# A hybrid decoder layer: stick quarters given out after the front step and after the rear step of each slot, in lumps of half the size

## What is computed

```
xn = RMSNorm(h); P = xn @ W_in
group A (RWKV-7, 8 heads x 64), for each token t:
    sa = S @ (-kk_t)
    S  = S * w_t + sa (kk_t * a_t)^T + v_t k_t^T
    y_t = S @ r_t
group B (stick-breaking, 8 heads x 64), for each block of 128 queries:
    z = q k^T / sqrt(64)
    A[t,s] = beta[t,s] * prod_{s<j<t} (1 - beta[t,j]), s < t, beta = sigmoid(z)
    o = A @ v
h += RMSNorm(concat(A, B) @ W_out)
h += RMSNorm(relu(RMSNorm(h) @ W_up)^2 @ W_down)
```

## Time and profile before

| | |
|---|---|
| median of 3 runs | 1838.2 us (1837.49 to 1838.92) |
| profiled execution | 1837.52 us, span 1835.6 us |
| PE busy | 1701.7 us, 93% of the span |
| DVE busy | 825.3 us, 45% |
| ACT busy | 699.3 us, 38% |
| POOL busy | 507.9 us, 28% |
| granted TensorE clock, mean | 0.968 |

### The profile page before, as it was taken

How to read it: one execution, slowest core, us unless ns; L and a number is a source line. 1 busy time by engine, 2 the same in 40 slices (tenths; PEclk the granted TensorE clock), 3 DMA queues, 4 the chain that set the end, 5 groups by cost and what they waited for, 6 DMA issues and landing times. The chain is left out here.

```text
span 1835.6 us, 36078 instructions
## 1 busy us (share of the span) xinstructions
PE 1701.7 (93%) x14676; PEld 1420.1 (77%) x14676; DVE 825.3 (45%) x1125; ACT 699.3 (38%) x1222; POOL 507.9 (28%) x523
## 2 busy tenths in 40 slices
PE   4999999969799999999992996999999999999998
PEld 4999999957677777877761784888888888888886
DVE  5132433325355455556549343444444444444436
ACT  5253443426456456555554343222121221212212
POOL 6332433304234333334425343111111111111110
PEclk7999999979899999999996997999999999999999
DMA  3336255341310300301012223211111111111104
GB/s 140 111 113 211 100 179 198 138 125 62 74 31 17 88 17 16 89 17 30 17 50 100 81 92 109 63 46 46 55 60 46 46 46 46 57 46 46 46 24 161
DMA packets 60890, 139.38 MB, mean 76 GB/s; under 512 B 5713, under 2 KB 32849, under 8 KB 60769
## 3 DMA queue, kind: packets, MB, share of 16 engines
q1 hardware_dynamic: 57024, 123.80, 21.0%
q10 hardware_dynamic: 3744, 13.85, 1.9%
HBM read 100.06 MB, written 37.57 MB: 75 GB/s over the span
## 5 line engine op out<-in xcount | busy, mean ns | idle before, releaser
L1722 POOL TENSOR_TENSOR ffn_ul<-ffn_relu,ffn_uh 128x512 fp32r<-128x512 f32 x64 | 82.8, 1294 | 576.2 <-ACT ffn_uh L1694 576.2
L1751 DVE TENSOR_TENSOR all_acc<-all_acc,ffn_down 128x512 f32<-128x512 f32 x240 | 161.2, 685 | 121.9 <-PE ffn_down L1798 121.3
L618 PE MATMUL inproj_acc<-xn_xh,inproj_wh 128*128 128x346 f32 (+1 forms) x624 | 207.4, 332 | 8.4 <-DVE inproj_wl L539 8.4
L1790 PE MATMUL ffn_up<-all_mh,ffn_wuh 128*128 128x512 f32 x512 | 200.1, 391 | 12.0 <-DVE ffn_wul L1734 12.0
L618 PE MATMUL inproj_acc<-xn_xh,inproj_wl 128*128 128x346 f32 (+1 forms) x624 | 201.1, 322 | 0.0
L618 PE MATMUL inproj_acc<-xn_xl,inproj_wh 128*128 128x346 f32 (+1 forms) x624 | 201.0, 322 | 0.0
L1798 PE MATMUL ffn_down<-ffn_wdh,ffn_uh 128*128 128x512 f32 x512 | 200.0, 391 | 0.0
L1790 PE MATMUL ffn_up<-all_ml,ffn_wuh 128*128 128x512 f32 x512 | 199.8, 390 | 0.0
L1790 PE MATMUL ffn_up<-all_mh,ffn_wul 128*128 128x512 f32 x512 | 199.6, 390 | 0.0
L1798 PE MATMUL ffn_down<-ffn_wdh,ffn_ul 128*128 128x512 f32 x512 | 199.4, 389 | 0.0
L1798 PE MATMUL ffn_down<-ffn_wdl,ffn_uh 128*128 128x512 f32 x512 | 199.2, 389 | 0.0
(11 more groups left out here) (244 smaller groups left out, 3442.8 us busy)
## 6 DMA issues: line engine op xcount, KB each, us to landing
ffn_raw_u<-in_w_up SPq DMA_DIRECT2D x32, 512.0 KB, 3.6
ffn_raw_d<-in_w_down SPq DMA_DIRECT2D x32, 512.0 KB, 4.2
xn_raw<-in_w_in SPq DMA_DIRECT2D x28, 512.0 KB, 4.6
p_scratch<-inproj_out ACTq DMA_DIRECT2D x26, 520.0 KB, 2.7
chunk_scratch<-inproj_fields SPq DMA_DIRECT2D x4, 2720.0 KB, 9.2
inproj_rkv<-p_scratch SPq DMA_DIRECT2D x14, 520.0 KB, 4.5
mix_fld<-chunk_scratch SPq DMA_DIRECT2D x17, 384.0 KB, 3.7
mix_fld<-chunk_scratch SPq DMA_DIRECT2D x17, 256.0 KB, 2.9
```

The costliest lines, as they stand in the source:

```text
L618: last = pe.matmul(acc[g][:, 0:size], w[s][:, kt, :], xx[:, kt, col:col + size], start=(kt == 0 and j == 0), stop=(kt == KD - 1 and j == 2))
L1722: pool.tensor_tensor(ul[s][:, f, cols], relu[j % 2][:, :], uh[s][:, f, cols].bitcast(F32), ALU.subtract).then_inc(u_low.sem, 1)
L1751: dve.tensor_tensor(part, part, downs[o % 4][:, :], ALU.add).then_inc(added.sem, 1)
L1790: last = pe.matmul(ups[j][:, :], w[f][:, k, :], xx[:, k, cols], start=(k == 0 and jj == 0), stop=(k == KD - 1 and jj == 2))
```

## The change

The quarters are given out after the front step and again after the rear step of each slot. There are twice as many lumps, of 1 or 2 quarters each (528 quarters over 288 half-slots). The same instructions are issued by each engine; only their order changes, and only on PE, ACT and DVE.

```
                 for _ in range(LAP_SLOTS):
-                    next(ahead, None)
-                    next(behind, None)
-                    k += 1
-                    due = k * quarters // slots
-                    for _ in range(due - given):
-                        next(sticks)
-                    given = due
+                    for part in (ahead, behind):
+                        next(part, None)
+                        k += 1
+                        due = k * quarters // (2 * slots)
+                        for _ in range(due - given):
+                            next(sticks)
+                        given = due
```

## The result

The changed kernel takes 1860.66 us (median of 4 runs, 1859.04 to 1863.29) against 1838.3 us before, a ratio of 1.0123 with a 95% interval of 1.0106 to 1.0141: 22.4 us slower. The forecast was 1866.2 us, 28 us slower, with 1854 to 1879 us as the range. Its profiled execution took 1859.04 us.

A forecast was written before the change was run, and what follows sets the result against it. PE was taken to bound the mixing stage. Profiled 1837.5 us, plus 37.1 for switches, less 9.1 for mix_a waits, DMA waits 0, gave 1865.5, and with 0.7 us 1866.2 us; range 1854 to 1879 us for 8 in 10.

The forecast's parts named there:

- The bound: Mixing stage: only PE is near its limit, busy 533.2 of 573.0 us, so its own time sets the stage.
- 109 added round trips: PE's order in the mixing stage: unbroken runs of 64-row matmuls go from 143 to 252.
- 0.34 us a trip: PE going from 128-row to 64-row matmuls and back: 0.34 us each, +37.1 us in all.
- The edges-alone case: PE's switches: only the two edges count, 0.19 us a trip; 1849.8 us in all, chance 6%.
- the rival by which handoffs were the bound: Mixing stage: apparent switch cost is handoff latency that finer order hides; faster, 1824.6 us, chance 3%.
- Waits for mix_a, -9.1 us: PE's waits for DVE's mix_a in the mixing stage: two thirds of 13.6 us go; bounds 0 and 13.6.
- The other reason: Mixing stage: half-lumps keep some matmuls between a tri sum and the rest sum needing its exponent; part of the 9.1 us.
- DMA waits, 0: PE's two stalls on loads of mix_vt for new pairs: no change, bounds -1 to +2 us.
- Lock-step lag: Mixing stage: DVE and ACT empty the rear bank later, 119 rear steps 0.1 us late each; 1878.1 us, chance 7%.
- the clock: PE in the mixing stage: many small gaps bring its clock down for a tenth of it; 1891 us, chance 5%.

The follow-up runs named there:

- the stage that held only this: Kernel before with a PE-only stage in front: 60 alternations of 64-row with 128-row matmuls took 20.93 us more than kind by kind.
- The two cuts of the lump: Kernel before with whole-tick lumps on all engines, ending after the tri sum or after the rest sum: 1845.89 us and 1845.43 us.
- the fewest trips: Kernel before with quarters given only after every second slot on all engines, 72 round trips: 1884.45 us.

## Why the prediction came out as it did

- **The bound.** Right: PE's own time sets the mixing stage, and outside of it nothing changed: the stage is 22.0 us longer and the span 21.6.
- **109 added round trips.** Right. Alone, 63 of them and 109 of them gave a loss in step with their number, and from ACT's and DVE's new order with PE's old to the changed kernel, which differ in PE's order alone, it is 32.7 us, 0.30 us a trip, with the waits that change beside them in it.
- **0.34 us a trip.** Right: 0.35 us in the stage that held only this, 0.355 in the row after. The edges-alone case (0.19) is out, and so is the rival by which handoffs were the bound (under 0.125). By the rule of the Trainium skill, TensorEngine Tiling (Array Packing), Key Properties, a change of tiling mode drains TensorE; the stage agrees, 0.35 us for a change of mode and under 0.01 for a change of matrices within one.
- **Waits for mix_a, -9.1 us.** About right, or up to 3 us too small; the forecast's distance of 5.5 us from the result lies here and in small waits that the sum put at nothing. The sum took two thirds of the matmuls' 13.6 us. But a matmul's modelled end lies 0.16 us beyond the start of the next in an unbroken stream (0.28 against 0.12 us for the L1232 at 934.14), so each wait loses that much in the table and short ones are not in it at all: the weight loads show 33 waits where the matmuls show 22. The loads' 24.4 us are somewhat too many, since they hold idle time that a load has without a wait too. A third reading takes starts: the distance from the matmul before, less the shortest that the same pair has in any of these runs at the same clock. These are 19.3 us in the same 33 places before and 10.4 in 16 after, 8.9 less. The matmul behind a wait is slow besides: from the one at 914.64 it is 0.34 us to the next start and not 0.23. PE's next row before:

```profile
914.98 0.39 PE L1218 MATMUL mix_cb<-mix_wsl,mix_rest_r 128*128 128x512 f32 x1
```

  By starts this second part is 2.9 us before and 0.4 after, which makes 11.4 us in all; the weight loads say 12.1. With the latter the sum comes to 37.1 - 12.1, less 1.6 for L1263's wait for mixed_o (2.1 to 0.5) and 1.0 for L1120's for mix_zi (1.4 to 0.4), plus 0.2 for mix_vt, or 22.6 us, and 22.4 were measured (21.5 between the two profiled executions). That it meets them so closely is in part luck, since it takes numbers from both tables; with 11.4 it is 23.3. The 3 to 6 us forecast for these waits by the matmuls after were too few; they are 8.6.
- **Why they fell.** Half right. ACT's half-lumps, which put its rear copy behind the exponential and the logarithm, are worth 9.2 us by themselves, as read from the earlier trace rows. The other reason, that half-lumps on PE keep small matmuls between tri and rest, is wrong: from ACT's and DVE's new order alone to the changed kernel only PE's order changes, and the waits for mix_a rise from 3.7 to 8.6 us; with PE's new order alone they are 42.7. The two cuts of the lump gave the same time as well. The prediction also took the order of all engines as one thing. It is two, with opposite signs, and the good one needs no round trip.
- **DMA waits, 0.** Right: +0.2 us in three stalls.
- **Lock-step lag and the clock.** Neither came in the changed kernel. The first exists: with a whole lump ahead of the rear copies PE stands some 30 us ahead of its steps. The second had its chance with 252 trips, and the clock stayed at 1.00 away from the DMA stalls. The up and down by idles between groups, of which the Trainium skill, TensorE: Matmul & The Clock Gate, A second HAM failure mode: psum-queue depth-cycling, tells, didn't come here. In other runs the clock fell after single waits of PE: with the fewest trips, 3.19 us for mix_a at 877.97, and 0.66 over the 10 us around it; with PE's order alone, 2.2 us for mix_zi at 905.04, and 0.60 over 906 to 910 us. The mean clock of the execution is 0.962 with the fewest trips and 0.965 with the whole lump between, against 0.968 before, so a part of these two losses is the clock.

## What to carry to other kernels

Where matmuls on half of TensorE's rows and columns share a queue with full ones, count the unbroken runs of each: here a return trip costs 0.35 us, so added trips need a gain that pays for them. Fewer trips alone won nothing either: 131 in place of 143 brought waits that cost more. The bound engine and the others wanted different orders, and the same merge function needn't order them alike. To split a reordering by engine and run each side alone is cheap, and showed a 10 us gain inside a 22 us loss. Price PE's waits from starts or from the weight loads' idle time; that of the matmuls, after modelled ends, gave 13.6 us where these gave 22.2 and 24.4.

## What was not expected of the hardware

In the stage made for it the cost is in the change between halved and full array: 240 full-array matmuls of another number kind and other weights, put between large ones in 60 groups, cost 0.40 us in all, while 240 pairs of halved ones cost 20.93 us. A matmul behind a wait is slower by about as much as the first large one behind small ones, 0.1 us. And a finer interleave, which made TensorE change between the two 504 times in 595 us, left its clock at 1.00 away from the stalls on loads.
